# Layer 1's expert weights: half of position 2's down into an unused 8 KB piece, the same piece again for position 15's gate, and another order of the first and last loads

## The chip, the cores and the metric

The kernel runs on one core of a Trainium2 chip. The metric is the device time of one execution in microseconds (us). Engines are named as in the profile: PE (TensorE matmul), PEld (its weight loads), DVE (VectorE), ACT (ScalarE), POOL (GpSimd), SP (SyncE, which here only issues DMAs).

## The reference, cut to what matters

Two layers over 256 latent and 256 context tokens of width 1024: modulation, attention in three branches, merge, then a mixture of experts. In layer 1, the last, only the 256 latent tokens go through the experts. The change touches the loading of their weights:

```
N_EXPERTS = 16; TOP_K = 2; D_FF_EXPERT = 512; D_MODEL = 1024
def _moe(h, w_router, router_bias, w_gate, w_up, w_down):
    combine = _route(hf, w_router, router_bias)      # weights of each token's two experts
    y = zeros_like(hf)
    for e in range(N_EXPERTS):
        a = silu(hf @ w_gate[e]) * (hf @ w_up[e])    # 1024 -> 512
        y = y + combine[:, e:e + 1] * (a @ w_down[e])  # 512 -> 1024
...
x = x + g2 * _moe(_modulate(x, norm2[l], sh2, sc2), ...)
return _rmsnorm(x, final_norm)
```

Everything is float32, so an expert's gate, up and down are 2048 KB each.

## The kernel before, in words

**Positions.** The 16 experts of a layer are worked off in 16 positions q, ordered by how many tokens they got; the program reads the experts of the later positions from `order`. A position gathers the rows of its tokens (POOL, indirect DMA into `hg`), PE transposes them, multiplies by gate and up (`up_gate`, lines 2358 and 2369 for a full position of 128 rows, line 2381 for one of 64), ACT and DVE form silu(gate) * up, PE transposes that (`transpose_a`) and multiplies by down (`down`, line 2399 full, 2405 otherwise). In layer 1 positions 6 and 11 are full. DVE scales the product into `yd` (line 1785), and POOL stores its rows to `y_d` in device memory. PE's order is up_gate(q), transpose of the rows of q + 1, down(q - 1), transpose_a(q); at q = 14 it is up_gate(14), rows of 15, down(13), transpose_a(14), down(14); then up_gate(15), half of the sums over the last two positions, transpose_a(15), down(15), three filling matmuls (line 2036), the other half of the sums (`add_position`, line 2042).

**Where weights lie.** The ring has 6 slots of 16 KB in each partition (2048 KB in all). In layer 1 gate and up rotate over three places: two pairs of slots, and for q % 3 == 2 a pair of spare places outside the ring, each in two pieces (X and WK for gate, KR and HT for up), where earlier data is dead. They are loaded in halves of 1024 KB (`load_half`, line 617). Down rotates over two slots (`load_expert`, line 598). The tile QR holds the attention's queries and results (24 KB for two latent tiles and two context tiles of three branches); in the experts of layer 1 its second 8 KB, columns 2048 to 4095, hold nothing until the end, when the outputs of the second latent tile are gathered there (`ygat[1]`).

**Who waits for whom.** All weight loads are issued by SP, in program order: one load whose wait is not yet met holds back all behind it. A load of gate or up waits for the matmuls that last read its place (`eg_mm`, `eu_mm`, position q - 3), a load of down for `ed_mm` of position q - 2. SP's program for layer 1: weights of attention and output projection; gate and up of positions 0 and 1; first halves of position 2; down 0 and 1 (they wait for the output projection); second halves of position 2; then, once the order of experts is known, for q = 3 to 14 gate and up of q and (from q = 4) down of q - 2; then down 13, down 14, gate and up of 15, down 15. PE waits in `weights` and `rest` for the semaphores of the pieces.

**The end.** When all rows are stored, POOL gathers each latent tile's two rows per token (lines 915 and 918) back. DVE adds the first tile's rows (line 1818), scales position 15's product (1785), adds the second tile's rows, then the last two positions' sums from PE (line 1899); then comes the final norm and the store.

Of the kernel before, what the change touches and what calls it, by code (L numbers as in the profile page):

```python
# [252 lines left out]
def build(nc, t_in, out):  # L253
# [7 lines left out]
    with ExitStack() as es:  # L261
# [3 lines left out]
        def sem(name):  # L265
# [46 lines left out]
        spare = [[W.rearrange("p (k n) -> p k n", k=KD // 2) for W in pair] for pair in (  # L312
            (X[:, NLAT:NT].rearrange("p a b -> p (a b)"), WK[:, 0:2 * D]),
            (KR[:, 2 * D:4 * D], HT[:, KD // 2:KD].rearrange("p a b -> p (a b)")))]
        wdown = [ring[:, s].rearrange("p a b -> p (a b)").rearrange("p (k n) -> p k n", k=4) for s in range(SLOTS)]
        qT = [QR[:, b * 4 * NT * P:(b + 1) * 4 * NT * P].rearrange("p (j n) -> p j n", j=4) for b in range(NB)]
        kT = [KR[:, 0:512].rearrange("p (j n) -> p j n", j=1), KR[:, 512:1024].rearrange("p (j n) -> p j n", j=1),
# [58 lines left out]
        def mod_out(l, j):  # L376

            if j < FIRST:
# [31 lines left out]
        HTf = HT[:, :, :].rearrange("p a b -> p (a b)")  # L410
        ygat = [[W[:, at + D * k:at + D * k + D] for k in range(2)]
                for W, at in ((HTf, 2 * D), (QR, 2 * D), (QR, 0), (KR, 2 * D))]
        add_bank = [(bank[1], bank[3])] + [(bank[6], bank[7])] * 3

        w_in_slot = [sem(f"w_in_slot{s}") for s in range(SLOTS)]
        w_in_spare = [sem(f"w_in_spare{j}") for j in range(2)]
        w_in_rest = [[sem(f"w_in_rest{i}{j}") for j in range(2)] for i in range(3)]
        vn_first = sem("vn_first")
        cleared = sem("cleared")
# [130 lines left out]
        def _(eng):  # L550
# [36 lines left out]
            def load_expert(l, q, e, j):  # L587
                n = NE * l + q - 1
                slot = place[l][3 * (q % 2) + j]
                if l == 0 and q == 0 and j == 0:  # L590
                    eng.wait_ge(gout_in, 32)
                    eng.wait_ge(modb_in, 64)
                if q < 2:
                    eng.wait_ge(*releases(held[l, slot][0]))
                else:
                    eng.wait_ge((eg_mm, eu_mm, ed_mm)[j], n * (2 if j == 2 else 1))
                dst = wdown[slot] if j == 2 else WR[slot]
                eng.dma_start(dst, expert_source(l, e, j)).then_inc(w_in_slot[slot], 16)

            def load_half(q, e, j, half):  # L600

                ks = slice(KD // 2 * half, KD // 2 * (half + 1))
                if half == 0:
                    if q >= 3:
                        eng.wait_ge((eg_mm, eu_mm)[j], NE + q - 2)
                    elif q == 2:
                        eng.wait_ge(pv_mm, before(att_pairs, L))
                    else:
                        eng.wait_ge(*releases(held[1, place[1][3 * q + j]][0]))
                if q == 2 and half:  # L610
                    eng.wait_ge(*((router_mm, 2 * L) if j else (rms_done, NT * 3 + NLAT)))
                if q % 3 == 2:
                    dst, first = spare[j][half], w_in_spare[j]
                else:
                    slot = place[1][3 * (q % 3) + j]
                    dst, first = WR[slot][:, ks], w_in_slot[slot]
                eng.dma_start(dst, expert_source(1, e, j)[:, ks]).then_inc(w_in_rest[q % 3][j] if half else first, 16)
# [59 lines left out]
            for l in range(L):  # L677
                biased_yet = False
                for i, (key, slot, prev, late) in enumerate(sections[l]):
                    if l == 0 and i <= FIRST:  # L680
                        continue
                    if late and not biased_yet:
                        load_biases(l)
                        biased_yet = True
                    if key == ("qa", 1):
                        for t in range(NT):
                            eng.wait_ge(ygat_in[t], 32)
                    load(key, slot, prev)
                for q in range(2):
                    load_pair(l, q, q)  # L690
                if l:
                    for j in range(2):
                        load_half(2, 2, j, 0)
                load_expert(l, 0, 0, 2)
                if l:
                    load_expert(l, 1, 1, 2)
                    for j in range(2):
                        load_half(2, 2, j, 1)
                eng.wait_ge(order_ready, l + 1)
                at = list(range(FIXED[l]))  # L700
                for q in range(2, NE):
                    if q >= FIXED[l]:
                        at.append(eng.value_load(order[0:1, q:q + 1], min_val=0, max_val=NE - 1))
                    lag = 2 if l else 1
                    if q == NE - 1:
                        for late in range(q - lag, q):
                            load_expert(l, late, at[late], 2)
                    if q >= FIXED[l]:
                        load_pair(l, q, at[q])
                    if 2 * lag <= q < NE - 1:  # L710
                        load_expert(l, q - lag, at[q - lag], 2)
                load_expert(l, NE - 1, at[NE - 1], 2)

                eng.wait_ge(flag_ready, l + 1)
                most = eng.value_load(flag[0:1, 0:1], min_val=0, max_val=NT * P)
                with eng.If(most > CAP):
                    q = sp[l]
                    for i in range(2):
                        eng.wait_ge(y_out[i], 16 * y_stores(l, NE - 2 + i))
                    with eng.Fori(0, NT - 1) as r:  # L720
                        with eng.Fori(0, NE) as e:
                            n = r * NE + e
                            eng.wait_ge(q["onehot"], n + 1)
                            for j in range(3):
                                dst = wdown[2] if j == 2 else WR[j]
                                eng.dma_start(dst, expert_source(l, e, j)).then_inc(q["w_in"], 16)
                    eng.wait_ge(q["w_in"], 48 * NE * (NT - 1))
                    eng.wait_ge(q["stored"], 16 * NE * (NT - 1))
# [8 lines left out]
        def _(eng):  # L737
# [42 lines left out]
            for l in range(L):  # L780
# [98 lines left out]
                def gather_outputs(table):  # L879

                    for t in range(nq):
                        for k in range(2):
                            eng.indirect_dma_start(ygat[t][k], None, table,
                                                   bass.IndirectOffsetOnAxis(ap=slot_g[:, k, t:t + 1], axis=0))\
                                .then_inc(ygat_in[t], 16)

# [22 lines left out]
                with eng.If(most <= CAP):  # L909
                    if l == 0:  # L910
                        gather_outputs(y_d[l][0:first_row(l, NE)])
                    else:
                        for t in range(nq):
                            for k in range(2):
                                dma(ygat[t][k], y_d[l][P * (nq * k + t):P * (nq * k + t + 1)]).then_inc(ygat_in[t], 16)  # L915

            eng.wait_ge(put_tr, 2)
            dma(modb[:, 0, 0], t_in["final_norm"].unsqueeze(0).broadcast_to([P, D])).then_inc(const_in, 16)
# [267 lines left out]
        def _(eng):  # L1186
# [160 lines left out]
            for l in range(L):  # L1347
# [466 lines left out]
                def add_gated(t):  # L1814

                    eng.wait_ge(ygat_in[t], 32 * (l + 1))
                    for i in range(2):
                        link(stt(X[:, t], ygat[t][i], r_w[:, t, i:i + 1], X[:, t], ALU.mult, ALU.add))  # L1818

                def first_rows(t):  # L1820

                    eng.wait_ge(ygat_in[t], 32 * (l + 1))
                    y0 = ygat[t][0]
                    if t < 2:
                        eng.wait_ge(add_mm, NT * l + t + 1)
                        for half in range(2):
                            cols = slice(CW * half, CW * half + CW)
                            ins = stt(y0[:, cols], y0[:, cols], r_w[:, t, 0:1], add_bank[t][half][:, :], ALU.mult, ALU.add)
                        link(ins)
                    else:  # L1830
                        link(ts(y0, y0, r_w[:, t, 0:1], None, ALU.mult))

                def second_rows(t):
                    y0, y1 = ygat[t]
                    link(stt(y0, y1, r_w[:, t, 1:2], y0, ALU.mult, ALU.add))

                def add_rows(t):

                    y0 = ygat[t][0]
                    link(tt(y0, y0, gout[:, t // NLAT], ALU.mult))  # L1840
                    ins = tt(X[:, t], X[:, t], y0, ALU.add)
                    if t < 2:
# [81 lines left out]
        def _(eng):  # L1924
# [121 lines left out]
            for l in range(L):  # L2046
# [286 lines left out]
                def weights(q, j):  # L2333
# [3 lines left out]
                        return [spare[j][k // (KD // 2)][:, k % (KD // 2)] for k in range(KD)]  # L2337
                    three = l and j < 2
                    slot = place[l][3 * (q % 3 if three else q % 2) + j]
                    eng.wait_ge(w_in_slot[slot], base[slot] + 16 * (q // (3 if three else 2) + 1))  # L2340
                    return [(wdown if j == 2 else WR)[slot][:, k] for k in range(4 if j == 2 else KD)]

                def rest(q, j):
# [214 lines left out]
```

## Time and profile before

| | us |
|---|---|
| median of 3 runs | 1608.92 (1606.95 to 1611.88) |
| the profiled execution | 1611.1 |
| its span | 1609.4 |
| PE busy | 1557.8 (97%) |
| DVE / ACT / POOL busy | 662.2 / 335.6 / 131.9 |
| DMA | 369.88 MB, mean 230 GB/s |

The profile is of one execution. The span is cut into 40 slices of about 40 us for the DMA line; a digit is the busy share in tenths. Times in the rows are us from the start of the span unless marked ns. A waiting engine costs time only where it sets the end.

### The profile page before, as it was taken

To read this page: it belongs to the slowest core of one execution; us is meant where nothing else is said; L and a number is where in the kernel's file an instruction comes from. 1 tells how busy PE (TensorE), PEld (TensorE's weight loads), DVE (VectorE), ACT (ScalarE), POOL (GpSimd) and SP (SyncE) were. 2 spreads that over 40 slices of the span, in tenths; PEclk is the share of its full clock that TensorE was granted. 3 is DMA by queue.
4 is the path that set the end of the run, shared out by engine and by line. 5 is a ranking of instruction groups with operands and counts; after the bars stand their busy time and mean duration, and the time that the engine had idled before them with its cause. 6 is when DMAs were issued, how large, how long until landed. Compare 5 with 4: busy or idle time off the path is not lost. (4 is left out here: it accounts for less than half of the span.)

```text
span 1609.4 us, 16272 instructions
## 1 busy us (share of the span) xinstructions
PE 1557.8 (97%) x6138; PEld 738.4 (46%) x6138; DVE 662.2 (41%) x1419; ACT 335.6 (21%) x776; POOL 131.9 (8%) x204
## 2 busy tenths in 40 slices
PE   8999999999999999899999999999999999989897
PEld 4444456644444444654444434446654445333332
DVE  2232067776677634611111126404766327211113
ACT  3011178810000011101011014115830012100001
POOL 1000001200000010000101020000210010111110
PEclk9999999999999999899999999999999998999999
DMA  9912120125535335499999797543139775999996
GB/s 341 302 56 104 65 67 2 40 91 163 186 140 209 105 95 232 162 335 363 407 398 409 276 383 265 157 170 118 29 126 343 272 289 221 384 410 407 412 376 283
DMA packets 109184, 369.88 MB, mean 230 GB/s; under 512 B 25155, under 2 KB 29395, under 8 KB 92628
## 3 DMA queue, kind: packets, MB, share of 16 engines
q1 hardware_dynamic: 96112, 330.32, 55.3%
q0 software_dynamic: 12560, 38.20, 6.6%
q8 instruction: 51, 0.84, 0.2%
q10 hardware_dynamic: 432, 0.29, 0.1%
q14 instruction: 29, 0.24, 0.0%
HBM read 360.97 MB, written 19.73 MB: 237 GB/s over the span
## 5 line engine op out<-in xcount | busy, mean ns | idle before, releaser
L2084 PE MATMUL bank<-ring_sb,HT_sb 128*128 128x512 f32 x384 | 168.5, 594 | 2.5 <-ACT HT_sb L959 2.5
L2111 PE MATMUL bank<-HT_sb,ring_sb 128*128 128x512 f32 x384 | 170.6, 596 | 0.0
L1248 DVE SCALAR_TENSOR_TENSOR MB_sb<-ring_sb,cT_sb,MB_sb 128x512 f32<-128x512 f32 x192 | 144.4, 752 | 6.8
L2381 PE MATMUL bank<-ring_sb,HT_sb 128*64 128x512 f32 x544 | 122.2, 602 | 0.7 <-ACT HT_sb L1129 0.7
L2111 PEld LDWEIGHTS bank<-HT_sb,ring_sb 128*128 128x128 f32 x384 | 72.1, 190 | 91.4 <-issue 91.3
L2084 PEld LDWEIGHTS bank<-ring_sb,HT_sb 128*128 128x128 f32 x384 | 71.7, 191 | 88.1 <-issue 88.1
L2405 PE MATMUL bank<-ring_sb,QR_sb 128*64 128x512 f32 x336 | 82.2, 634 | 16.1 <-DMA ring_sb<-w_e_down 13.5
L2081 PE MATMUL bank<-HT_sb,ring_sb 128*128 128x512 f32 (+1 forms) x256 | 97.4, 539 | 0.0
L1092 ACT ACTIVATE WK_sb<-bank 128x512 f32<-128x512 f32 x36 | 21.5, 597 | 341.9 <-PE bank L2111 232.1
L2118 PE MATMUL bank<-QR_sb,ring_sb 128*128 128x512 f32 x192 | 86.3, 593 | 0.0
L2110 PE MATMUL bank<-ring_sb,HT_sb 128*128 128x512 f32 x192 | 85.4, 596 | 0.7 <-issue 0.7
L1462 DVE TENSOR_REDUCE nmx_sb<-bank 128x1 f32<-128x512 f32 (+1 forms) x48 | 26.5, 596 | 136.4 <-PE bank L2161 136.4
L2399 PE MATMUL bank<-ring_sb,QR_sb 128*128 128x512 f32 x176 | 77.9, 596 | 1.4 <-DMA ring_sb<-w_e_down 1.4
L1770 DVE TENSOR_TENSOR QR_sb<-QR_sb,bank 64x512 f32<-64x512 f32 x21 | 21.9, 1043 | 138.5 <-ACT QR_sb L1139 138.5
L2161 PE MATMUL bank<-KR_sb,QR_sb 64*128 64x512 f32 (+1 forms) x288 | 70.6, 569 | 4.2 <-ACT MB_sb L1083 3.0
L2381 PEld LDWEIGHTS bank<-ring_sb,HT_sb 128*64 128x64 f32 x544 | 39.1, 139 | 72.2 <-issue 70.9
L2358 PE MATMUL bank<-ring_sb,HT_sb 128*128 128x512 f32 x160 | 71.0, 597 | 1.2 <-ACT HT_sb L1126 1.2
L2132 PEld LDWEIGHTS bank<-tab_sb,MB_sb 128*128 128x128 f32 x480 | 51.5, 141 | 44.6 <-issue 42.0
L2369 PE MATMUL bank<-ring_sb,HT_sb 128*128 128x512 f32 x160 | 70.4, 593 | 0.0
L2081 PEld LDWEIGHTS bank<-HT_sb,ring_sb 128*128 128x128 f32 x256 | 48.3, 191 | 45.0 <-issue 43.4
L2132 PE MATMUL bank<-tab_sb,MB_sb 128*128 128x128 f32 x480 | 68.2, 281 | 0.6 <-DVE MB_sb L1448 0.4
L1768 DVE TENSOR_TENSOR QR_sb<-QR_sb,bank 128x512 f32<-128x512 f32 x11 | 11.6, 1054 | 137.6 <-PE bank L2369 85.4
(358 smaller groups left out, 1908.2 us busy)
## 6 DMA issues: line engine op xcount, KB each, us to landing
ring_sb<-w_e_down SPq DMA_DIRECT2D x32, 2048.0 KB, 15.0
ring_sb<-w_mod SPq DMA_DIRECT2D x24, 2048.0 KB, 9.3
ring_sb<-w_in SPq DMA_DIRECT2D x21, 2048.0 KB, 14.2
ring_sb<-w_e_gate SPq DMA_DIRECT2D x16, 2048.0 KB, 11.7
ring_sb<-w_e_up SPq DMA_DIRECT2D x16, 2048.0 KB, 12.4
ring_sb<-w_e_gate SPq DMA_DIRECT2D x22, 1024.0 KB, 17.6
ring_sb<-w_e_up SPq DMA_DIRECT2D x22, 1024.0 KB, 18.5
ring_sb<-w_branch SPq DMA_DIRECT2D x8, 1024.0 KB, 13.4
```

The costliest lines, as they stand in the source:

```text
L1248: link(stt(a, WR[slot][:, k], cT[:, k, strm:strm + 1], a, ALU.mult, ALU.add))
L2081: ins = mm(bank[j % 4][:, 0:w], WR[slot][:, k, P * t:P * t + P], HT[:, k, 0:w], start=(k == 0), stop=(k == KD - 1))
L2084: ins = mm(bank[j % 4][:, :], HT[:, k, P * t:P * t + P], WR[slot][:, k], start=(k == 0), stop=(k == KD - 1))
L2110: return mm(dst[:, :], HT[:, k, P * t:P * t + P], WR[slot][:, k], start=(k == 0), stop=(k == KD - 1))
L2111: return mm(dst[:, :], WR[slot][:, k, P * t:P * t + P], HT[:, k], start=(k == 0), stop=(k == KD - 1))
L2118: return mm(dst[:, :], w[:, P * t:P * t + P], qT[n][:, k], start=(k == 0), stop=(k == 3))
L2132: ins = mm(bank[3 + side][:, P * k:P * k + P], probs[(2 * p + side) % NPROB][:, P * k:P * k + P], ident, start=True, stop=True, is_transpo ...
L2161: mm(sbank[(2 * p + side) % 4][:, w], qT[b][part, j, P * t:P * t + P], kT[b][part, j if b == N else 0, w], start=True, stop=True).then_inc ...
L2358: ins = mm(bank[0][:, :], hgT[q % 2][:, k], gate[k], start=(k == 0), stop=(k == KD - 1))
L2381: ins = mm(bank[0][HALF * side:HALF * side + HALF, :], hgT[q % 2][:, k, 0:HALF], w[k], start=(k == 0), stop=(k == KD - 1))
L2399: ins = mm(bank[4 + half][:, :], eaT[:, k], w[k][:, CW * half:CW * half + CW], start=(k == 0), stop=(k == 3))
L2405: ins = mm(bank[4][HALF * half:HALF * half + HALF, :], eaT[:, k, 0:HALF], w[k][:, CW * half:CW * half + CW], start=(k == 0), stop=(k == 3))
```

## The change

A new view `extra` of QR's second 8 KB (in each partition; 1024 KB in all) serves two loads under a semaphore of its own, `w_in_extra`: the first half of position 2's down, issued behind the gate and up of positions 0 and 1, and later the first half of position 15's gate, once down(2) is done. Position 2's down loads only its other half into the ring slot. The first halves of position 2's gate and up are issued in front of positions 0 and 1. At the end of the stream, SP's order becomes: first half of gate 15, down 13, first half of up 15, second halves of gate and up 15, down 14, down 15. The outputs of the second latent tile are gathered into QR's first 8 KB instead of its second. PE, ACT and DVE keep their order of work; PE takes the pieces from their new places.

```diff
+        extra = QR[:, 2 * D:4 * D]
+        extra_gate = extra.rearrange("p (k n) -> p k n", k=KD // 2)
+        extra_down = extra.rearrange("p (k n) -> p k n", k=2)
...
+        def gathered(l, t):
+            return ygat[NLAT if l and t else t]
...
             def load_expert(l, q, e, j):
...
-                eng.dma_start(dst, expert_source(l, e, j)).then_inc(w_in_slot[slot], 16)
+                source = expert_source(l, e, j)
+                if (l, q, j) == (1, 2, 2):
+                    dst, source = dst[:, 2:4], source[:, 2:4]
+                eng.dma_start(dst, source).then_inc(w_in_slot[slot], 16)
...
             def load_half(q, e, j, half):
                 ks = slice(KD // 2 * half, KD // 2 * (half + 1))
+                if (q, j, half) == (NE - 1, 0, 0):
+                    eng.wait_ge(ed_mm, 2 * (NE + 3))
+                    eng.dma_start(extra_gate, expert_source(1, e, j)[:, ks]).then_inc(w_in_extra, 16)
+                    return
...
+                if (q, j, half) == (NE - 1, 0, 1):
+                    eng.wait_ge(eg_mm, NE + q - 2)
...
                     load(key, slot, prev)
+                if l:
+                    for j in range(2):
+                        load_half(2, 2, j, 0)
                 for q in range(2):
                     load_pair(l, q, q)
                 if l:
-                    for j in range(2):
-                        load_half(2, 2, j, 0)
+                    eng.wait_ge(branch_mm, before(merge_jobs, L))
+                    eng.dma_start(extra_down, expert_source(1, 2, 2)[:, 0:2]).then_inc(w_in_extra, 16)
                 load_expert(l, 0, 0, 2)
...
                     lag = 2 if l else 1
+                    if l and q == NE - 1:
+                        load_half(q, at[q], 0, 0)
+                        load_expert(l, q - 2, at[q - 2], 2)
+                        load_half(q, at[q], 1, 0)
+                        load_half(q, at[q], 0, 1)
+                        load_half(q, at[q], 1, 1)
+                        load_expert(l, q - 1, at[q - 1], 2)
+                        continue
...
 # TensorE, weights(q, j)
+                    if (l, q, j) == (1, NE - 1, 0):
+                        eng.wait_ge(w_in_extra, 32)
+                        return [extra_gate[:, k] if k < KD // 2 else WR[slot][:, k] for k in range(KD)]
                     eng.wait_ge(w_in_slot[slot], base[slot] + 16 * (q // (3 if three else 2) + 1))
+                    if (l, q, j) == (1, 2, 2):
+                        eng.wait_ge(w_in_extra, 16)
+                        return [extra_down[:, k] if k < 2 else wdown[slot][:, k] for k in range(4)]
```

## Rows read from the trace of the kernel before

**Rows 1.** The page, parts 1 and 2: PE's share, and DMA by slices.
```profile
PE 1557.8 (97%) x6138; PEld 738.4 (46%) x6138; DVE 662.2 (41%) x1419; ACT 335.6 (21%) x776; POOL 131.9 (8%) x204
...
DMA  9912120125535335499999797543139775999996
```

**Rows 2.** Waits of PE from 1100 to 1610 us: total, times, longest.
```profile
PE bank L2405 <- DMA ring_sb<-w_e_down: 13.5, 4, 5.4
...
PE bank L2399 <- DMA ring_sb<-w_e_down: 1.4, 1, 1.4
```

**Rows 3.** Stretches: length, busy of PE, PEld, DVE, ACT, POOL, clock, DMA share, GB/s.
```profile
1391.00:1561.00 170.00, 155.04 (x653) 58.65 (x653) 24.62 (x35) 13.48 (x23) 21.75 (x22) 0.96 1.01 408
...
1561.00:1566.00 5.00, 4.93 (x32) 2.11 (x32) 1.60 (x2) 1.19 (x2) 0.00 (x0) 1.00 0.47 193
1566.00:1588.00 22.00, 21.19 (x106) 8.00 (x104) 3.26 (x6) 1.19 (x2) 2.03 (x2) 1.00 0.96 391
```

**Rows 4.** PE in order of time: down of positions 3, 4, 8, 11, 12.
```profile
1415.78 3.65 PE L2405 MATMUL bank<-ring_sb,QR_sb 128*64 128x512 f32 x16 [1.53 <-DMA ring_sb<-w_e_down]
...
1432.89 6.56 PE L2405 MATMUL bank<-ring_sb,QR_sb 128*64 128x512 f32 x16 [5.04 <-DMA ring_sb<-w_e_down]
...
1498.42 6.23 PE L2405 MATMUL bank<-ring_sb,QR_sb 128*64 128x512 f32 x16 [5.43 <-DMA ring_sb<-w_e_down]
...
1546.48 7.13 PE L2399 MATMUL bank<-ring_sb,QR_sb 128*128 128x512 f32 x16 [1.43 <-DMA ring_sb<-w_e_down]
...
1561.74 3.65 PE L2405 MATMUL bank<-ring_sb,QR_sb 128*64 128x512 f32 x16
```

**Rows 5.** SP's issues: gate 2, down 2, down 12 to 14, last half 15.
```profile
1309.96 0.46 SPq L617 DMA_DIRECT2D X_sb<-w_e_gate  x1
...
1382.99 0.34 SPq L598 DMA_DIRECT2D ring_sb<-w_e_down  x1
...
1536.88 28.91 SPq L598 DMA_DIRECT2D ring_sb<-w_e_down  x3
...
1567.55 0.41 SPq L617 DMA_DIRECT2D ring_sb<-w_e_up  x1
```

**Rows 6.** Issue to landing, us (last column): down 12, down 14, last half 15.
```profile
ring_sb<-w_e_down SPq DMA_DIRECT2D x1, 2048.0 KB, 24.8
...
ring_sb<-w_e_down SPq DMA_DIRECT2D x1, 2048.0 KB, 8.3
...
ring_sb<-w_e_up SPq DMA_DIRECT2D x1, 1024.0 KB, 16.4
```

**Rows 7.** Stretches behind the waits at down 4 and down 8.
```profile
1432.00:1438.00 6.00, 5.11 (x12) 1.48 (x14) 0.00 (x0) 0.00 (x0) 0.00 (x0) 0.50 1.00 415
...
1498.00:1504.00 6.00, 5.58 (x14) 1.63 (x16) 0.00 (x0) 0.00 (x0) 0.00 (x0) 0.53 1.03 429
```

**Rows 8.** PE from 1576 us: transposes 14, down 14, down 15, filling, sums.
```profile
1576.95 0.46 PE L2306 MATMUL bank<-tab_sb,QR_sb 64*128 64x64 f32 x4
1578.22 3.65 PE L2405 MATMUL bank<-ring_sb,QR_sb 128*64 128x512 f32 x16 [0.81 <-DVE QR_sb L1791]
...
1591.52 3.65 PE L2405 MATMUL bank<-ring_sb,QR_sb 128*64 128x512 f32 x16 [0.56 <-issue]
1595.10 2.84 PE L2036 MATMUL bank<-tab_sb 128*128 128x512 f32 x6
1597.88 1.99 PE L2042 MATMUL bank<-KR_sb,MB_sb 64*128 64x512 f32 x8
```

**Rows 9.** DVE at the end: first tile's rows, product 15, the sums.
```profile
1594.22 2.61 DVE L1818 SCALAR_TENSOR_TENSOR X_sb<-HT_sb,r_w_sb,X_sb 128x1024 f32<-128x1024 f32 x2 [2.81 <-DMA HT_sb<-y_d]
...
1596.86 0.69 DVE L1785 TENSOR_TENSOR KR_sb<-bank,MB_sb 128x512 f32<-128x512 f32 x1
...
1600.56 2.61 DVE L1899 TENSOR_TENSOR X_sb<-X_sb,bank 128x512 f32<-128x512 f32 x4 [0.24 <-DVE X_sb L1818]
```

**Rows 10.** The stretch between the loads of position 2 and down 0.
```profile
1330.00:1340.00 10.00, 10.00 (x33) 4.89 (x31) 5.23 (x5) 0.60 (x1) 0.54 (x1) 1.00 0.13 53
```

More of the change, by code:

```diff
@@ L416, in build @@
         w_in_spare = [sem(f"w_in_spare{j}") for j in range(2)]
+        w_in_extra = sem("w_in_extra")
         w_in_rest = [[sem(f"w_in_rest{i}{j}") for j in range(2)] for i in range(3)]
@@ L882, in gather_outputs @@
                         for k in range(2):
-                            eng.indirect_dma_start(ygat[t][k], None, table,
+                            eng.indirect_dma_start(gathered(l, t)[k], None, table,
                                                    bass.IndirectOffsetOnAxis(ap=slot_g[:, k, t:t + 1], axis=0))\
@@ L914, in _ @@
                             for k in range(2):
-                                dma(ygat[t][k], y_d[l][P * (nq * k + t):P * (nq * k + t + 1)]).then_inc(ygat_in[t], 16)
+                                dma(gathered(l, t)[k], y_d[l][P * (nq * k + t):P * (nq * k + t + 1)]).then_inc(ygat_in[t], 16)
             eng.wait_ge(put_tr, 2)
@@ L1817, in add_gated @@
                     for i in range(2):
-                        link(stt(X[:, t], ygat[t][i], r_w[:, t, i:i + 1], X[:, t], ALU.mult, ALU.add))
+                        link(stt(X[:, t], gathered(l, t)[i], r_w[:, t, i:i + 1], X[:, t], ALU.mult, ALU.add))
                 def first_rows(t):
                     eng.wait_ge(ygat_in[t], 32 * (l + 1))
-                    y0 = ygat[t][0]
+                    y0 = gathered(l, t)[0]
                     if t < 2:
@@ L1833, in second_rows @@
                 def second_rows(t):
-                    y0, y1 = ygat[t]
+                    y0, y1 = gathered(l, t)
                     link(stt(y0, y1, r_w[:, t, 1:2], y0, ALU.mult, ALU.add))
                 def add_rows(t):
-                    y0 = ygat[t][0]
+                    y0 = gathered(l, t)[0]
                     link(tt(y0, y0, gout[:, t // NLAT], ALU.mult))
```

## The prediction

> **What bounds the kernel now.** I read the page's busy shares first: PE is busy 97% of the span, and the DMA line shows full slices from the 34th on [rows 1]. So PE sets the time nearly everywhere, and the question is who makes it idle in layer 1's experts. The waits of PE name one line: down's matmuls wait for `w_e_down`, 13.5 us in 4 waits, and 1.4 us once more at the full position [rows 2]. Then the table of stretches: from 1391 to 1561 us the 16 DMA engines are busy all the time (share 1.01, 408 GB/s), so this is a stretch that the weight stream bounds, and PE is only as early as its weights [rows 3]. PE's order of work shows where: down(3) starts 1.53 us late, down(4) 5.04, down(8) 5.43, down(11) 1.43 [rows 4]. From down(4) at 1432.89 to down(12) at 1561.74 lie 8 positions of 6 MB (2048 KB each for gate, up and down; I call 1024 KB one MB): 48 MB in 128.85 us, 2.68 us per MB with the row gathers and stores of POOL's queue among them. After a wait PE also pays for its clock: down(4) takes 6.56 us and down(8) 6.23, where down(3), behind a wait of 1.53, takes 3.65 [rows 4]; the granted clock in those stretches is 0.50 and 0.53, that is mostly 1.2 GHz instead of 2.4 [rows 7]. While the stream bounds, this costs nothing more: the next late down waits for its landing either way.
>
> After 1561 it is different. The DMA share falls to 0.47 for 5 us [rows 3], and PE runs on with waits under 1 us: down(13), the transposes of position 14 until 1577.41, down(14) at 1578.22 (0.81 late, on a DVE copy), up and gate of 15, down(15) at 1591.52, the three filling matmuls, the last sums from 1597.88 [rows 8].
>
> **The change part by part.**
>
> 1. Half of down(2) moves ahead. It is now issued with the loads at 1308 to 1310, in front of the routing, and SP's load at 1382.99 carries 1 MB instead of 2 [rows 5]. In that place the DMA engines have room: the share is 0.13 from 1330 to 1340 [rows 10]. The new wait for the last branch product asks for nothing later than what load_pair(1) just in front of it has waited for. Everything behind 1382.99 in the stream lands one MB earlier. One MB is 2.5 us by the last pair (below) and 2.68 by the mean with POOL's traffic, which is not removed; I take 2.5. For this the stream must never run dry; by rows 3 it doesn't before 1561. So down(3) loses its wait, down(4) starts at 1430.4, down(12) at 1559.2, and PE is 2.5 us ahead there. One more DMA to issue (0.33 to 0.5 us on SP [rows 5]) and one more semaphore wait on PE lie beside waits that SP and PE have anyway: nothing.
>
> The Trainium skill ("DMA: Bandwidth & Descriptors", Specifications) gives an HBM limit of about 358 GB/s for a core; by that page one MB would be 2.93 us and the head start would be an estimated 2.9. The trace shows 408 GB/s over 170 us [rows 3], so the measurement decides.
>
> 2. Position 2's first halves of gate and up are issued first, some 47 us before the present 1309.96 [rows 5], right behind w_out. Their place has been free since attention. They push position 0's first half back by 2 MB, 5 us; it is first used by position 0 behind the routing, long after the nearly idle 1330 to 1340. The batch at 1308 gets 2 MB less and the 1 MB of part 1, and the engines are nearly idle behind it either way [rows 10]. Nothing gained, nothing lost. The same holds for the gathers into QR instead of the second half: same size, same place in POOL's queue, and the last rows of hg have been transposed long before.
>
> 3. The last loads. Before, the stream's order is down(12), down(13), down(14), the four halves of 15, down(15): the down loads are issued from 1536.88, the last one at 1565.46 because it waits for down(12)'s matmuls, and 15's halves behind it until 1567.55 [rows 5]. Now it is down(12), gate half 15 (into the free piece), down(13), the other three halves of 15, and only then down(14). PE's order is unchanged: it wants down(14) before up and gate of 15. Down(14) therefore has 4 MB more in front of it. Before, it lands at 1565.46 + 8.3 = 1573.8, 3.6 us before PE is ready for it. The last half of 15 lands at 1567.55 + 16.4 = 1584.0 [rows 6]. What has landed by then before is exactly what has to land up to down(14) now, less the one MB: 1584.0 - 2.5 = 1581.5. From the other side: down(12) landed at 1536.88 + 24.8 = 1561.7 [rows 6], now 1559.2, and 8 MB follow: at 2.5 us 1579.2, at 2.68 us 1580.7. I take 1581.4, next to the count that rests on the real landings, with 1579.2 as the lower end. The 0.47 share does not contradict this: a load lands when its last engine is through, and in those 5 us some engines still work without a break, those that are behind. That the slow ones run on through is shown by the landings: 10 us for the four halves, none missing in between.
>
> PE comes to down(14) at 1577.41 - 2.5 = 1574.9 (down(13) is no hindrance: 1559.2 + 3 x 2.68 = 1567.2, wanted at 1570.9). It waits 6.5 us for 1581.4. Then the clock: waits of 5.04 and 5.43 us cost 2.91 and 2.58 us in the 16 matmuls behind them [rows 4]. At half clock each further us of waiting uses up a us of the low stretch, worth 0.5: 2.58 - 0.5 x 1.1 = 2.0 us here (ends: 0 and 2.9). Down(14) ends at 1581.4 + 3.65 + 2.0, and everything behind it on PE is 1581.4 + 2.0 - 1578.22 = 5.2 us later than before.
>
> 4. The tail gives some back. PE's last sums run from 1597.88; the first is done about 1598.9 (half of 1.99 us), and DVE takes it at 1600.56 [rows 8, 9]: 1.65 us of slack. DVE until then is held by its chain: first rows at 1594.22, 15's product at 1596.86, second rows, then the sums. The stores and gathers in front of the first rows hang on down(13), which is 2.5 us earlier, so now DVE waits for down(15), ending at 1595.1 + 5.2 = 1600.3; product 0.7, rows 2.6, gaps 0.4: sums at 1604.0. Both ways the end moves by 5.2 - 1.65 = 3.5 us.
>
> **The sum.** The profiled execution took 1611.1 us (span 1609.4), the median of the runs shown is 1608.92; I add the difference to the median. Part 1: -2.5 (PE at the end of down(13)). Part 3: +5.7 for the landing (from 2.5 early to 3.2 late at down(14)), +2.0 for the clock. Part 4: -1.65 of slack. Part 2: 0. Net +3.5, **1612.4 us**. With the ends of landing and clock it is -0.7 (1579.2, clock untouched: 1.0 - 1.65) to +4.6 (1581.5, 2.9); its own range with the scatter of runs (1606.95 to 1611.88) is 1609 to 1615.
>
> **The rivals.**
>
> A. The idle share is usable. If the early halves of 15 fill the engines that stand idle from 1561 to 1566, the mean share counts: (1 - 0.47) x 5 = 2.6 us, down(14) lands at 1578.8. PE waits 3.9 us, between the 1.5 that left the clock alone and the 5.04 that didn't; without a fall it is 0.6 us late, 1.0 ahead at the end: 1607.9. For it: the share is real. Against it: the engines that are behind have no gap, and a landing waits for them.
>
> B. Down(14) lands before PE wants it, as before. Then the 2.5 us stay: 1606.4, or a little less, since up and gate of 15 no longer run close behind their landing. It would need loads that overtake; against it, the landings come in the order of issue: 1561.7, 1573.8, 1584.0 [rows 5, 6].
>
> The Trainium skill ("DMA: Bandwidth & Descriptors", Queues, rings and completion order) has a rule for B: completion is not first in, first out for an issuing engine, since a copy on one DMA engine can finish ahead of an earlier one on all 16. By it down(14) could overtake and the time be 1606.4; no run here shows such a copy among the weight loads, whose landings keep their order.
>
> C, the slow side. The early MB is eaten: if the stream runs dry once between 1383 and 1561 because a slot comes free no sooner, down(12) is at 1561.7 again, and down(14) lands at 1584.0. PE then is 5.8 late and 2.0 for the clock, less 1.65: +6.2, 1615.1. It decides from the point where the last 4 halves are in front of down(14), which the order sets in any case; for it speaks that issues depend on PE's progress, against it that a load lies in the queue far longer than 2.5 us: down(12) lands 24.8 us after its issue [rows 6], of which its own 2 MB are 5.
>
> **Chances.** Forecast 0.55, A 0.15, B 0.13, C 0.17. With 2 us of scatter around each, and 0.3% being 4.8 us (what a measurement of this kernel can tell from no change): the forecast's 0.55 splits into 0.39 within and 0.16 slower; A is within (0.14) but for 0.01; B 0.06 within, 0.07 faster (there are waits and low clock in the stretch that this execution may show better than others); C 0.01 within, 0.16 slower. Together faster 0.08, same 0.60, slower 0.32. The range 1606.3 to 1616.2 reaches to B on one side and over C on the other.
>
> **What would show it.** In the new trace: no wait at down(3); down(4) and down(8) still late, some 2.5 us earlier in time; down(12) near 1559.2; then one wait of 5 to 7 us on PE at down(14) for `w_e_down`, low clock behind it, none at position 15; a DMA share near 1 between 1561 and 1566. If down(14) starts by 1576, B is true and parts 1 and 3 both paid; if down(12) is at 1561.7, C. The prediction is wrong at its root if loads of one queue don't land in the order of their issue.

## The result, and the profile after

The changed kernel takes 1614.12 us (median of 9 runs, 1612.23 to 1617.62) against 1610.46 for the kernel before in the same measurements (9 runs, 1606.95 to 1615.43). The ratio is 1.0025, 95% interval 1.0014 to 1.0037: 4.0 us slower, 2.3 to 6.0. The prediction was 3.5 us slower (1612.4, counted from a median of 1608.92 in three runs). The changed kernel's profiled execution took 1613.59 us, span 1611.9.

PE's waits from 1100 us on, in the trace after (us in total, times, longest):

```profile
PE bank L2438 <- DMA ring_sb<-w_e_down: 16.4, 5, 6.3
...
PE bank L2432 <- DMA ring_sb<-w_e_down: 2.2, 2, 1.9
```

These answer to [rows 2]: with a megabyte less in the stream, PE waits more for down, not less (18.6 us against 14.9); 4.27 us of it are one new wait at down 14. Lines have moved: down is now 2438 and 2432. PE in order of time, after: down of positions 3, 4, 8, 11, 12, then 14, and the tail:

```profile
1413.26 3.65 PE L2438 MATMUL bank<-ring_sb,QR_sb 128*64 128x512 f32 x16
...
1428.17 5.04 PE L2438 MATMUL bank<-ring_sb,QR_sb 128*64 128x512 f32 x16 [2.83 <-DMA ring_sb<-w_e_down]
...
1494.91 5.81 PE L2438 MATMUL bank<-ring_sb,QR_sb 128*64 128x512 f32 x16 [6.28 <-DMA ring_sb<-w_e_down]
...
1543.03 8.83 PE L2432 MATMUL bank<-ring_sb,QR_sb 128*128 128x512 f32 x16 [1.89 <-DMA ring_sb<-w_e_down]
...
1559.84 3.65 PE L2438 MATMUL bank<-ring_sb,QR_sb 128*64 128x512 f32 x16
...
1579.78 6.04 PE L2438 MATMUL bank<-ring_sb,QR_sb 128*64 128x512 f32 x16 [4.27 <-DMA ring_sb<-w_e_down]
...
1595.47 3.65 PE L2438 MATMUL bank<-ring_sb,QR_sb 128*64 128x512 f32 x16 [0.56 <-issue]
1599.05 2.84 PE L2063 MATMUL bank<-tab_sb 128*128 128x512 f32 x6
1601.83 1.99 PE L2069 MATMUL bank<-KR_sb,MB_sb 64*128 64x512 f32 x8
```

The wait at down(3) is gone [rows 4]; down(14) has a new one of 4.27 us and runs at low clock where it stood 0.81 us on a DVE copy [rows 8]. Absolute times mix in what happened before the experts, so I measure each trace from SP's issue of position 3's first load, the first one behind the routing. In the trace before it stands at 1365.76, in the one after at 1364.55:

```profile
1365.76 0.34 SPq L617 DMA_DIRECT2D ring_sb<-w_e_gate  x1
```
```profile
1364.55 0.34 SPq L633 DMA_DIRECT2D ring_sb<-w_e_gate  x1
```

Counted from there, in us (each is a start in PE's timeline less that issue; end is the span less it):

| kernel | down 4 | down 8 | down 11 | down 12 | down 14 | last sums | end |
|---|---|---|---|---|---|---|---|
| before | 67.13 | 132.66 | 180.72 | 195.98 | 212.46 | 232.12 | 243.64 |
| after | 63.62 | 130.36 | 178.48 | 195.29 | 215.23 | 237.28 | 247.35 |
| difference | -3.5 | -2.3 | -2.2 | -0.7 | +2.8 | +5.2 | +3.7 |

These are single executions. Two traces of one kernel (experiment 1) differ in this count by 0.2 to 0.5 us up to down 11, and by about 2 us at down 12 and at the end.

The early megabyte brings its 2.3 to 3.5 us to the late downs, loses most of it between down(11) and down(12), and the order of the last loads takes more than all of it. Issue to landing in the trace after (last column, us) of down 12, issued at 1532.96, of the last half of 15, at 1553.32, and of down 14, at 1563.56:

```profile
ring_sb<-w_e_down SPq DMA_DIRECT2D x1, 2048.0 KB, 24.9
...
ring_sb<-w_e_up SPq DMA_DIRECT2D x1, 1024.0 KB, 21.5
...
ring_sb<-w_e_down SPq DMA_DIRECT2D x1, 2048.0 KB, 16.2
```

Down 12 lands at 1557.9, the last half of 15 at 1574.8, down 14 at 1579.8, where PE starts (1579.78). The stretches after (length, busy time of PE, PEld, DVE, ACT, POOL, clock, DMA share, GB/s):

```profile
1391.00:1561.00 170.00, 155.71 (x664) 59.39 (x662) 24.79 (x36) 14.08 (x24) 21.75 (x22) 0.96 1.01 410
1561.00:1566.00 5.00, 5.00 (x26) 1.67 (x24) 1.02 (x2) 0.00 (x0) 0.92 (x1) 1.00 1.00 411
...
1579.00:1585.00 6.00, 5.22 (x14) 1.62 (x16) 0.00 (x0) 0.00 (x0) 0.00 (x0) 0.53 0.56 227
```

The idle share of 1561 to 1566 [rows 3] is filled, as intended by the new order, and it helps nobody: PE is given more idle time 14 us later. The idle share hasn't gone either, it has moved. Before, down 13 is in flight from 1553.65 to 1568.0; after, down 14 from 1563.56 to 1579.8, and the load behind it (down 15, which waits for down 13's matmuls) is issued only at 1575.19. Both times some engines are done with the load several us before it lands, first before, then after:

```profile
1563.00:1566.00 3.00, 3.00 (x18) 1.10 (x16) 0.54 (x1) 0.00 (x0) 0.00 (x0) 1.00 0.35 145
```
```profile
1574.00:1576.00 2.00, 1.51 (x10) 0.46 (x6) 0.80 (x2) 0.00 (x0) 0.00 (x0) 1.00 0.34 143
```

### The profile page after: what moved, and what is told of

It is laid out like the page before. It is cut to its first block, busy times and chain, and to the rows that moved or that the text cites. A ratio compares the mean times of both kernels' runs of the same rounds, so it can differ in the third digit from the quotient of the medians.

```text
span 1611.9 us, 16274 instructions
## 1 busy us (share of the span) xinstructions
PE 1556.7 (97%) x6138; PEld 734.0 (46%) x6138; DVE 661.6 (41%) x1419; ACT 335.6 (21%) x776; POOL 131.8 (8%) x204
## 4 chain that ended last, share of the span: by engine, by line
PE 85%; DMA 9%; DVE 3%; ACT 1%; issue 1%; SPq 0%; POOL 0%; DVEq 0%; POOLq 0%; ACTq 0%
PE bank L2138 10%; PE bank L2111 10%; DMA ring_sb<-w_e_down 8%; PE bank L2108 6%; PE bank L2414 5%; PE bank L2137 5%; PE bank L2145 5%; PE bank L2291 5%; PE bank L2432 4%; PE bank L2438 4%; PE bank L2391 4%; PE bank L2402 4%; PE bank L2178 4%; PE bank L2188 4%; PE bank L2159 4%; PE bank L2144 3%
```

## Experiments

**1 to 4: which part does what.** The first takes the changed kernel and moves one load.

```diff
                     if l and q == NE - 1:
                         load_half(q, at[q], 0, 0)
                         load_expert(l, q - 2, at[q - 2], 2)
+                        load_expert(l, q - 1, at[q - 1], 2)
                         load_half(q, at[q], 1, 0)
                         load_half(q, at[q], 0, 1)
                         load_half(q, at[q], 1, 1)
-                        load_expert(l, q - 1, at[q - 1], 2)
                         continue
```

> The changed kernel with one load moved: SP issues down 14 right behind down 13, and the three remaining halves of position 15 behind it. Theory (the place of down 14 in the stream costs what the early megabyte gains, and more): down 12 still lands near 1559.5 on the trace, down 14 before PE asks for it at about 1576, no wait there and no low clock behind it, and the last half of 15 lands about 1581, before PE's second half of up and gate of 15. The time falls about 2.3 us below the kernel before, ratio 0.9985, and 6 us below the changed one. Rival (the cost is in the first part, the loads moved in front of the routing, or in the piece's two uses): down 14's place is no matter, the time stays within 1 us of the changed kernel, ratio 1.0025.

Measured: 1609.19 us, ratio to the kernel before 0.9992 (0.9980 to 1.0003), and run again later on another chip 1608.90 us, 0.9982 (0.9967 to 0.9997). Down(14) in its trace:

```profile
1577.48 0.46 PE L2333 MATMUL bank<-tab_sb,QR_sb 64*128 64x64 f32 x4
1578.74 3.65 PE L2438 MATMUL bank<-ring_sb,QR_sb 128*64 128x512 f32 x16 [0.81 <-DVE QR_sb L1818]
```

No wait for the weights, full clock. One load's place is the whole of the loss: the intervals of this kernel and of the changed one don't touch. That it is also faster than the kernel before, only the second measurement tells. The gain is smaller in the first run than the 2.3 us expected, and the trace says where (its first load of position 3 is at 1367.05): down 12 comes at 195.21, no earlier than in the changed kernel, since down(11) ran at low clock here too. In the trace of the second measurement (first load of position 3 at 1363.09) it ran at full clock:

```profile
1541.04 7.13 PE L2432 MATMUL bank<-ring_sb,QR_sb 128*128 128x512 f32 x16 [1.39 <-DMA ring_sb<-w_e_down]
```

There down 12 comes at 193.16 and the end at 240.11, 3.5 us ahead of the kernel before, against 242.05 and 1.6 in the first.

> The kernel with down 14 in front of the halves once more, on one chip with the two below, so that the fillings are compared with it under the same conditions. Expected: ratio to the kernel before 0.9990, 0.9980 to 1.0000. If it comes out at 0.9981 too, the fillings at down 11 and down 8 have done nothing that the times can show.

It came out at 0.9982, so the fillings below, whose best ratio is 0.9981, have done nothing that the times can show.

The second is the kernel before with the early half alone:

```diff
...
                     for j in range(2):
                         load_half(2, 2, j, 0)
+                    eng.wait_ge(branch_mm, before(merge_jobs, L))
+                    eng.dma_start(extra_down, expert_source(1, 2, 2)[:, 0:2]).then_inc(w_in_extra, 16)
                 load_expert(l, 0, 0, 2)
...
+                if (l, q, j) == (1, 2, 2):
+                    dst, source = dst[:, 2:4], source[:, 2:4]
...
```

> The kernel before with nothing but half of position 2's down loaded early into the free piece; the last loads and the first ones in the old order. Theory: one megabyte less behind 1383 us is 2.5 us for everything that waits for the stream: no wait at down 3, down 12 near 1559.3, the rest of PE 2.5 us earlier, ratio 0.9985 (2.3 us). Rival C (the stream runs dry somewhere, the megabyte is eaten): down 12 near 1561.7, ratio 1.000. Rival (the old order profits from the fuller queue less than PE's shift): the last half of 15, landing near 1581.5, holds up PE at 15, ratio 0.9995.

Measured: 1609.33 us, 0.9989 (0.9976 to 1.0001). From position 3's first load: down 4 at 64.08, down 8 at 130.82, down 12 at 194.46, end 241.81: 3.0, 1.8, 1.5 and 1.8 us before the kernel before. The sign and the place are as expected, the size reaches the end at about three quarters in the trace; the interval of the times still holds 1. Position 15 was not held up.

The third is the kernel before with the new order of the last loads alone, in the old places:

```diff
                     lag = 2 if l else 1
+                    if l and q == NE - 1:
+                        load_half(q, at[q], 0, 0)
+                        load_expert(l, q - 2, at[q - 2], 2)
+                        load_half(q, at[q], 1, 0)
+                        load_half(q, at[q], 0, 1)
+                        load_half(q, at[q], 1, 1)
+                        load_expert(l, q - 1, at[q - 1], 2)
+                        continue
```

> The kernel before with nothing but the new order of the last loads (gate half 15, down 13, the other halves of 15, down 14, down 15), all in their old places in the ring. Theory: down 14 lands where the last half of 15 landed before, 1584.0; PE waits 6.6 us there, 2.0 us of low clock behind it, 1.65 us of slack in the tail: 6.2 us above the kernel before, ratio 1.0038. By the difference of the changed kernel (+3.7 instead of my +3.5) it may be 5.5 to 6.5. Rival A (the DMA engines that stood idle from 1561 to 1566 take the halves): down 14 lands near 1581, ratio 1.002. Rival (the order costs nothing, the piece does): ratio 1.000.

Measured: 1615.88 us, 1.0033 (1.0020 to 1.0047), 5.3 us slower. Its down(12) and down(14):

```profile
1560.25 3.65 PE L2413 MATMUL bank<-ring_sb,QR_sb 128*64 128x512 f32 x16
...
1581.54 6.62 PE L2413 MATMUL bank<-ring_sb,QR_sb 128*64 128x512 f32 x16 [5.62 <-DMA ring_sb<-w_e_down]
```

Counted from its first load of position 3 (1364.12), down 14 starts at 217.42; expected were 218.2. The wait is 5.62 and the low clock costs 2.97; the end is at 250.08, 6.4 us behind the kernel before, 6.2 expected. Here all 16 DMA engines are busy from 1561 to 1566 as well (share 1.02), so rival A is out: filling the idle share does not bring the last load of the queue forward by anything near 2.6 us.

The fourth keeps the changed kernel and its order, and gives PE something to do in the new wait:

```diff
                 def down(q):
                     n = NE * l + q
+                    if (l, q) == (1, NE - 2):
+                        fill_wait(4)
```

> The changed kernel with four filling matmuls (about 0.95 us each) on PE between the transposes of position 14 and down 14, where it waits 4.27 us on the trace. Theory: the landing stays where it is (1579.8), but the clock doesn't fall, so down 14's 16 matmuls take 3.65 us and not 6.04: 2.4 us below the changed kernel, ratio to the kernel before 1.001. Rival (the landing of a later load or the tail's DVE chain takes over, so that the clock costs nothing): the gain is under 0.7 us, ratio 1.0022.

Measured: 1612.28 us, 1.0005 (0.9992 to 1.0017), some 3 us below the changed kernel by the two ratios, whose intervals overlap (1.0014 to 1.0037 there). In its trace (a float32 matmul has two records, so x8 is four fillings, and x16 at down is eight matmuls):

```profile
1578.39 3.70 PE L2063 MATMUL bank<-tab_sb 128*128 128x512 f32 x8
1584.54 5.29 PE L2440 MATMUL bank<-ring_sb,QR_sb 128*64 128x512 f32 x16 [2.44 <-DMA ring_sb<-w_e_down]
```

The landing hardly moves (214.33 from the first load, 215.23 in the trace after). But the clock was low in this execution too, behind the 2.44 us that were left of the wait; the matmuls take 5.29 us and not 3.65. So the expected 2.4 us were not tested: the trace gives the clock 0.75 us (6.04 - 5.29), and the 3 us of the ratios are hardly more than the 0.22% by which two measurements of one kernel differ below. What the low clock costs at down 14 rests on the traces themselves, 6.04 and 6.62 us for matmuls that take 3.65, with everything behind them on PE later by it.

**5: the first loads.** The kernel before with position 2's first halves in front of positions 0 and 1.

```diff
+                if l:
+                    for j in range(2):
+                        load_half(2, 2, j, 0)
                 for q in range(2):
                     load_pair(l, q, q)
-                if l:
-                    for j in range(2):
-                        load_half(2, 2, j, 0)
```

> The kernel before with nothing but position 2's first halves of gate and up issued in front of positions 0 and 1. My theory from the prediction: the DMA engines have room on both sides, so nothing is gained or lost, ratio 1.000 (0.9990 to 1.0010). Rival (the two megabytes behind w_out hold up something in front of the routing: the stores of the modulation or the projection): up to 5 us late loads, ratio above 1.001, and the first load of position 3's weights comes later on the trace.

Measured: 1610.86 us, 0.9999 (0.9987 to 1.0011), end at 243.12. Nothing, as expected.

**6: one megabyte more.** The kernel of the first experiment, where position 3's down is loaded by half and the rest is stale data; so its output is not the reference's.

```diff
-                if (l, q, j) == (1, 2, 2):
+                if (l, q, j) in ((1, 2, 2), (1, 3, 2)):
                     dst, source = dst[:, 2:4], source[:, 2:4]
```

> The kernel with down 14 in front of the halves, and the first half of position 3's down is not loaded at all, so that one megabyte more is missing from the stream (position 3's outputs are computed from stale data). It tells how much of a megabyte reaches the end. Theory if the stream bounded to the end: 2.5 us more, ratio 0.9977. Theory as the last traces have it (down 12 follows down 11 with no wait, PE bounds from there): down 4, 8 and 11 start 2.5 us earlier, their waits shrink, down 8's from 6.2 to 3.7 or, since PE gets ahead, stays, and the end gains 1.5 to 2.5 us. Rival (PE bounds already): nothing, ratio 0.9992.

Measured: 1606.20 us, 0.9959 (0.9945 to 0.9974; 6 runs), that is 3.7 us below the 0.9982 of its base and 5.3 below the 0.9992. In the trace (first load of position 3 at 1369.38) down 4 starts at 60.77 with no wait, down 8 at 127.72, down 11 at 176.57, the end is at 240.42: 2.8, 2.5, 1.8 and 1.6 us ahead of the base. The trace's part is within the expected 1.5 to 2.5, the times give more. Against the second trace of the base, down 4, 8 and 11 are 2.6, 2.0 and 1.4 us ahead and the end is 0.3 us behind: down(11) took 8.77 us at low clock here and 7.13 there. So the stream still bounds up to down 11, and a further early megabyte is worth something there; how much of it reaches the end, between nothing and 5 us, is open.

**7 to 11: the clock inside the stream.** The changed kernel and the one with down 14 in front both ran down(11) in 8.83 us behind a wait of 1.8 to 1.9, where [rows 4] has 7.13 behind 1.43. I put filling matmuls in front of late downs, on a bank that only full positions use. This is the one with two in front of down 11; the others have `{8: 5}`, `{8: 5, 11: 2}` and `{4: 2, 8: 5, 9: 1, 11: 1}` in its place:

```diff
                 def down(q):
                     n = NE * l + q
+                    if l and q in {11: 2}:
+                        for _ in range({11: 2}[q]):
+                            mm(bank[1][:, :], ident, tab[:, 0:CW], start=True, stop=True)
```

> The kernel with down 14 in front of the halves, plus two filling matmuls (1.85 us together) on PE in front of down 11, where it waited 1.78 us and then ran its 16 matmuls in 8.83 us at low clock instead of 7.13. Theory (behind down 11 PE, not the stream, sets the time: down 12 starts with no wait, so what the clock takes at down 11 is lost for good): down 11 takes 7.13, the end comes 1.7 us earlier in executions in which the clock would have fallen, ratio to the kernel before about 0.9985 against 0.9992 without the filling. Rival, the sentence of my prediction (the next late down waits for its landing anyway): no change, ratio 0.9992.

Measured: 1609.13 us, 0.9981 (0.9970 to 0.9992); down(11) takes 7.03, end at 241.78. Against 0.9992 and 0.9982 for the same kernel without the filling this is no difference that can be told.

> The kernel with down 14 in front of the halves, plus five filling matmuls (4.6 us together) on PE in front of down 8, where it waited 6.22 us and then took 5.82 us instead of 3.65. Theory: here the stream bounds, down 9 and down 11 still wait for their landings, so the 2.2 us of clock come back as a longer wait at down 9 and nothing is gained: down 8 at 3.65 us, the wait at down 9 up from 1.74 to about 3.9, down 11 at the same time, ratio 0.9992. Rival (the low clock costs everywhere): 2.2 us less, ratio 0.9978.

Measured: 1608.99 us, 0.9983 (0.9971 to 0.9995). PE in order of time, down 8 and down 9, first without the filling, then with it:

```profile
1497.23 5.82 PE L2438 MATMUL bank<-ring_sb,QR_sb 128*64 128x512 f32 x16 [6.22 <-DMA ring_sb<-w_e_down]
...
1513.22 3.65 PE L2438 MATMUL bank<-ring_sb,QR_sb 128*64 128x512 f32 x16 [1.74 <-DMA ring_sb<-w_e_down]
```
```profile
1489.06 4.56 PE L2423 MATMUL bank<-tab_sb 128*128 128x512 f32 x10
1495.49 3.65 PE L2441 MATMUL bank<-ring_sb,QR_sb 128*64 128x512 f32 x16 [1.86 <-DMA ring_sb<-w_e_down]
...
1511.54 5.26 PE L2441 MATMUL bank<-ring_sb,QR_sb 128*64 128x512 f32 x16 [3.96 <-DMA ring_sb<-w_e_down]
```

Down(8) saves its 2.2 us, the wait at down(9) grows by 2.2, and down(9) now pays with its own clock, 5.26 against 3.65. Inside the stream a gain of PE goes into the next wait, here to the tenth of a microsecond.

The count from position 3's first load fails in this trace: the end is at 245.81, 3.8 us behind the same kernel without the filling. This load was early and position 1 behind it late (PE waited 3.39 us for DVE there, and its granted clock was 0.50 from 1366 to 1370), so the DMA engines stood idle from 1374 to 1378 (share 0.01) before the next loads could be issued. SP's first load of position 3 and its down 2:

```profile
1359.89 0.34 SPq L633 DMA_DIRECT2D ring_sb<-w_e_gate  x1
...
1381.57 0.34 SPq L608 DMA_DIRECT2D ring_sb<-w_e_down  x1
```

Counted from down 2 the end is at 224.13, and 224.69 and 222.69 in the two traces without the filling. Counted so, the changed kernel ends 3.4 us behind the kernel before (229.82 against 226.41) and the early half alone 2.4 us ahead of it (223.99), so the readings above stand.

> The same with five filling matmuls in front of down 8 and two in front of down 11. Theory: only the clock at the last late down (9 or 11, whichever PE runs on from without another wait) reaches the end, worth 0 or 1.7 us by execution; the filling at down 8 moves its 2 us into the next wait. Ratio to the kernel before about 0.9983, the same as with down 11 alone. Rival (every low clock costs): 0.9970.

Measured: 1612.56 us, 1.0005 (0.9992 to 1.0017). A miss: neither 0.9983 nor the rival's 0.9970. In its trace the experts take what they take in the others (241.62 from position 3's first load to the end), but this load stands later than in any other (1370.21 is the next):

```profile
1372.98 0.34 SPq L633 DMA_DIRECT2D ring_sb<-w_e_gate  x1
```

> The kernel with fillings at down 8 and 11 once more: its first run stood at 1.0005 where 0.9983 was expected, and its trace lost the time in front of the experts (position 3's weights issued at 1372.98 us, 1363 to 1367 in its neighbours), in code that no edit of mine touches. If that was chance of the executions, it comes out at about 0.9983 now and the first load near 1366. If it belongs to the build, the ratio is again 1.0000 or more, with some 6 us lost in front of the experts, and a difference of 0.2% between two builds can't be put down to an edit by its time alone.

Measured: the same kernel at 0.9983 (0.9970 to 0.9996), with that load at 1365.37 and 242.03 behind it. So it was not the build, and 12 runs and a 95% interval did not cover what it was: 0.22% between two measurements of one kernel. The second was on another chip; the first shared its chip with two kernels that came out at 0.9981 and 0.9982. Nor does the late load explain the median of 1612.56: the traced execution, 1616.26 us, was the slowest of the twelve, and the first loads of the other traces lie between 1359.89 and 1370.21, not 1363 and 1367 as the expectation has it.

> The same with fillings in front of every late down: two at 4, five at 8, one at 9, one at 11. Theory: no low clock between down 4 and the tail, down 9 takes 3.65 us and not 5.35, so PE reaches down 11 before its landing in every execution and goes on from there at full clock: the best of these kernels, ratio to the kernel before about 0.9980. Rival (the fillings at 4 and 9 delay PE where a load is already there, by up to 0.9 us each): above 0.9985.

Measured: 1608.34 us, 0.9981 (0.9969 to 0.9992). The time is the expected one, the reason is not. Low clock was still there: down(6) took 8.83 us behind a wait of 2.16, down(9) 6.44 behind what its one filling left:

```profile
1509.73 6.44 PE L2441 MATMUL bank<-ring_sb,QR_sb 128*64 128x512 f32 x16 [3.77 <-DMA ring_sb<-w_e_down]
```

End at 242.82, no better than 240.11 and 242.05 in the two traces without fillings. No time and no trace shows a gain from these fillings at the end.

## Why the prediction was right, point by point

**Part 1, the early half: right in mechanism, a little large at the end.** 2.5 us were expected for everything behind the old place of the load. The landing of down 12 moved from 1561.7 to 1557.9, from position 3's first load by 2.6 us. What the prediction did not see is that PE no longer follows it: "the next late down waits for its landing either way" holds up to down(11), the last late one. There the changed kernel ran at low clock and lost 1.7 us (8.83 against 7.13), and down(12) had no wait left to hide it in; it started 1.9 us behind its landing. So PE came to down(14) at 1575.52 instead of 1574.9, counted from the first load 1.8 us later than predicted. In this kernel that cost nothing, since the wait at down(14) took it in (4.27 us, not 6.5); in the kernel with down 14 in front it takes as much again from the gain in one of two traces (down 12 at 195.21 instead of 193.16).

**Part 2: right.** The first loads' order alone: 0.9999.

**Part 3, the landing of down 14: right.** The count "what has landed by the last half of 15, less one megabyte" gave 1581.4, that is 215.6 from position 3's first load (at 1365.76); measured 215.23. With nothing but the order changed it gave 218.2, measured 217.42. The three loads of 15 in front of down 14 land at 1574.8 at the latest, first used behind 1585: they are early by 10 us, and down 14 late by 4. Counting by an old landing has one strength that the prediction doesn't name: some engines finish a load several us before it lands, and a landing in the old trace has that delay in it, while a count by the mean share (rival A) leaves it out.

**The clock: 2.0 expected, 2.39 measured** (6.04 - 3.65). The prediction let a longer wait use up the low stretch; the wait was shorter, and the cost, by the same 0.5 per us, should have been 3.2 (2.58 + 0.5 x 1.16). The runs show 2.97 behind 5.62 and 2.39 behind 4.27, and behind waits of 5.37, 5.40 and 5.43 (early half alone at down 8, new order alone at down 4, kernel before at down 8) the low clock costs 1.68, 1.61 and 2.58. So these traces show no such rule; that the term came out near is luck within its bounds (0 to 2.9, and 2.97 is a hair outside). The upper end of the sum is +4.5, not +4.6 (1581.5 - 1578.22 + 2.9 - 1.65).

**Part 4, the tail: right.** PE's last sums start 5.16 us later (5.2), the end 3.71 later (3.5). DVE in the trace after, last rows of the chain:

```profile
1599.22 0.69 DVE L1812 TENSOR_TENSOR KR_sb<-bank,MB_sb 128x512 f32<-128x512 f32 x1 [0.28 <-PE bank L2438]
1599.83 2.59 DVE L1845 SCALAR_TENSOR_TENSOR X_sb<-QR_sb,r_w_sb,X_sb 128x1024 f32<-128x1024 f32 x2
...
1603.00 2.60 DVE L1926 TENSOR_TENSOR X_sb<-X_sb,bank 128x512 f32<-128x512 f32 x4 [0.58 <-PE bank L2069]
```

Before, the gathered rows held it up and PE's sums lay ready [rows 9]; now it waits for PE at both places, as the sum assumed.

**Rivals.** A is out by the third experiment, B by the landing at 1579.8, C by down 12's. None of the 65 weight loads from position 3's first on overtook an earlier one in the trace after, and none of 64 before, so the Trainium skill's rule ("DMA: Bandwidth & Descriptors", Queues, rings and completion order) found no case here. The rule is about a later copy on one engine beside an earlier one on all 16; down 14 is no such copy, so the rule did not speak for B as the prediction has it. The page's limit of 358 GB/s (the Trainium skill, same page, Specifications) does not hold in this kernel either: 410 GB/s over 170 us.

**Open.** Why the clock falls behind a wait of 1.78 us in one execution and not behind 2.20 in another was not settled. Nor what part of the 3 us between the changed kernel with and without four fillings is clock and what is chance, nor why one kernel measured 1.0005 and 0.9983.

## What to carry to other kernels

In a queue that never runs dry a load's place is its time: before moving one, list the loads in the order in which they are wanted, and take none that is wanted later past one that is wanted sooner, even if the sooner one can't be issued yet and engines stand idle meanwhile. A load can be timed for the new order by counting bytes: find the load behind which the same bytes have landed in the old trace. And an early load pays only up to the last place where the consumer waits; from there on the consumer's own work, its clock included, sets the time.

## What the runs showed that I had not expected

The granted clock also falls behind short waits: down(11) ran at low clock behind 1.89, 1.78 and 1.79 us (8.83, 8.83 and 8.77 us for matmuls that take 7.13), and at full clock behind 1.39, 1.43, 2.20 and 2.02. Nor does the length of the wait decide in positions of 64 rows: down(4) took 3.65 us behind 3.00 (early half alone) and 5.35 behind 2.33 (two fillings at down 11). The share of the DMA engines drops to 0.34 while down 14 is still 4 to 6 us from its landing, and did so before with down 13 (0.35): the engines do not finish a load together, and the last one counts. Why some are behind was not looked at. And two measurements of one kernel, 12 runs each and each beside the kernel before, gave 1.0005 and 0.9983: a difference of 0.2% can't be put down to an edit by its time alone. The trace's own count from a fixed point helps, but the point has to lie behind what varies: from position 3's first load it missed by some 4 us in one trace, from down 2's issue it did not.
